# Weight pieces of a mixture-of-experts layer, issued by one queue or by two

## The chip, the cores and the metric

The kernel runs on one core of a Trainium2 chip. Its engines are named as in the profile: PE is TensorE (matrix products), DVE is VectorE, ACT is ScalarE, POOL is GpSimd and SP is SyncE, which here only waits and issues DMAs. A DMA that SP or ACT issues is carried out by the core's 16 DMA engines. The metric is the time of one execution in microseconds (us) of device time; less is better.

## The reference

One decoder layer for 256 tokens of width 1024, in float32: two attention mixers with gates, then a mixture of experts, then a final norm. Nearly all the bytes are in the experts. Each token goes to 4 of 32 experts, and each expert has three matrices of 1024 x 1024:

```python
def expert_block(args):
    xb, e = args
    g = xb @ w_gate[e] + b_gate[e]
    u = xb @ w_up[e] + b_up[e]
    g = jnp.minimum(g, SWIGLU_LIMIT)
    u = jnp.clip(u, -SWIGLU_LIMIT, SWIGLU_LIMIT)
    a = g * jax.nn.sigmoid(SWIGLU_ALPHA * g) * (u + 1.0)
    return a @ w_down[e] + b_down[e]
```

That is 32 x 3 x 4 MiB = 402.7 MB of expert weights, each byte read once, out of the 437.7 MB that the profile counts as read from memory.

## The kernel before

The first part (to about 228 us of the span) computes norms, projections, attention and the router. It is not touched. The second part runs over the 32 experts. An expert's tokens are gathered into 64 slots, and its three products are made on PE (line 1044), with the weights as the moving operand.

The weights come in **pieces** of 2 MiB: piece n is half of one matrix, 128 partitions with one run of 16 KB each. An expert has 6 pieces (gate 0 and 1, up 2 and 3, down 4 and 5), so there are 192, numbered 0 to 191. The order is given by the table ORDER: expert by expert, except that the last two experts have gate and up of both first, and then the two down matrices: pieces 188 and 189 for expert 30, 190 and 191 for expert 31. Piece 191 is cut into three DMAs.

The pieces go round a ring of 10 buffers (`RING = 10`): piece n lies in buffer n modulo 10. In the trace the buffers have the names pool (seven of them), attn, slot_wv and slot_gt; even buffers are pool_51, slot_wv, pool_50, pool_53 and slot_gt, odd ones attn, pool_49, pool_52, pool_54 and pool_55. Each buffer has its own semaphore `ld_ring`, on which PE waits before it uses the piece. When PE has finished a piece it adds one to `pieces_used`, and piece n may be issued when `pieces_used` is n - 9 or more.

Pieces 0 to 9 are issued by SP during the first part, as their memory falls free (line 369). All others are issued by SP in a loop (lines 421 to 428), in the order of n, each after its wait; so all pieces stand in one queue.

For every expert n, ACT does this, in this order: the sigmoid of the gate (`item_sigmoid`, line 621, after the gate product), the copy of the gathered tokens of expert n + 1 (`gathered_out`, line 629), for some experts the copy of a turned selection (line 625), the copy of the turned activation (`turned_activation`, line 634, which PE needs for the down product), and two copies of the expert's output (`item_out`, line 641, after the down product). The function `five` (line 644) writes this out for five experts; it is called six times, for experts 0 to 29, and `last_pair` does experts 30 and 31.

PE's order for an expert: gate product, gather of the next expert's rows (line 980), up product, turning of the gathered rows (line 700), combination of older outputs (line 1063), turning of the activation (line 700), down product. A product is 32 matmuls, 16 for each piece.

Of the kernel before, what the change touches and what calls it, by code (L numbers as in the profile page):

```python
# [35 lines left out]
E = 32  # L36
# [3 lines left out]
PIECES = 6  # L40
RING = 10
# [3 lines left out]
ORDER = [(e, m, j) for e in range(LAST) for m in range(3) for j in range(2)]  # L45
# [72 lines left out]
def layer(nc, x, ln_mix_g, w_in, b_gate_a, b_gate_b, w_o_a, w_o_b, w_out, ln_ffn_g, w_router, b_router,  # L118
# [6 lines left out]
    def sem(name):  # L125
        return ctx.enter_context(nc.semaphore(name))

    with ctx:
# [70 lines left out]
        ring = [attn[:, 8 * SEQ:24 * SEQ].rearrange("p (k c) -> p k c", c=D), slot_wv]  # L199
        ring = [pool[2]] + ring + [pool[0], pool[1], pool[3], pool[4], pool[5], slot_gt, pool[6]]  # L200
# [60 lines left out]
        ld_ring = [sem(f"ld_ring{s}") for s in range(RING)]  # L261
# [27 lines left out]
        pieces_used = sem("pieces_used")  # L289
# [17 lines left out]
        expert_v = [t[0].rearrange("e (j p r) f -> e j p r f", p=P, r=RUN) for t in (w_gate, w_up, w_down)]  # L307
# [48 lines left out]
        def _(sp):  # L356
# [61 lines left out]
            sp.wait_ge(prob_ready, NB)  # L418
            for q in range(4):
                sp.dma_start(b_dn[q], b_down[0][:, SEQ * q:SEQ * q + SEQ]).then_inc(ld_bdn, 16)  # L420
            for n in range(RING, E * PIECES):
                sp.wait_ge(pieces_used, n - RING + 1)
                if n == E * PIECES - 1:
                    for q, r in enumerate((slice(0, 2), slice(2, 3), slice(3, 4))):
                        sp.dma_start(ring[n % RING][:, r, :], expert_v[2][E - 1, 1][:, r, :]).then_inc(ld_last[q], 16)
                else:
                    expert, m, j = ORDER[n]
                    sp.dma_start(ring[n % RING][:], expert_v[m][expert, j]).then_inc(ld_ring[n % RING], 16)
# [32 lines left out]
        def _(act):  # L461
# [33 lines left out]
            for c in range(8):  # L495
                for b in range(NB):
# [6 lines left out]
                    else:  # L503
                        at, n = V_CHUNKS[c]
# [114 lines left out]
            def item_sigmoid(n):  # L619
                act.wait_ge(g_ready, n + 1)  # L620
                act.activation(sig, g_act, ACT.Sigmoid, scale=ALPHA).then_inc(sig_done, 1)  # L621

            def turned_selection(groups, slots=P, bank=DN):
                act.wait_ge(sel_turned, groups)
                act.activation(sel_t[0:slots], ps[0:slots, bank, 0:SEQ], ACT.Copy).then_inc(sel_t_ready, 1)

            def gathered_out(n):
                act.wait_ge(gathered, n + 1)
                act.activation(x_rows, ps[:, X, :], ACT.Copy).then_inc(x_rows_ready, 1)

            def turned_activation(n, dst=a_t):
                act.wait_ge(a_turned, n + 1)

                act.activation(dst.rearrange("p (h j) c -> p j h c", h=2),  # L634
                               ps[:, G, :].rearrange("p (j h c) -> p j h c", h=2, c=SLOTS), ACT.Copy)\
                   .then_inc(a_t_ready, 1)

            def item_out(n, side, y_group):
                act.wait_ge(pieces_used, n * PIECES + 6)
                for h in range(2):  # L640
                    act.activation(y_group[SLOTS * side:SLOTS * side + SLOTS, 512 * h:512 * h + 512],  # L641
                                   ps[SLOTS * h:SLOTS * h + SLOTS, DN, :], ACT.Copy).then_inc(y_ready, 1)

            def five(t):
                for j, members in enumerate(MEMBERS):
                    for side, i in enumerate(members):
                        n, group = t * FIVE + i, t * len(MEMBERS) + j
                        if n == 0:
                            act.wait_ge(prob_turned, 1)
                            act.activation(prob_t, ps[0:E, DN, 0:SEQ], ACT.Copy).then_inc(prob_t_ready, 1)  # L650
                        item_sigmoid(n)
                        gathered_out(n + 1)
                        if side == 0 and group:
                            turned_selection(group, SLOTS * len(MEMBERS[j - 1]))
                        turned_activation(n)
                        item_out(n, side, y_bufs[Y_OF[j]])

            def last_pair():
                item_sigmoid(LAST)
                gathered_out(LAST + 1)  # L660
                turned_selection(GROUPS - 1, SLOTS)
                turned_activation(LAST)
                item_sigmoid(LAST + 1)
                turned_selection(GROUPS, bank=X)
                turned_activation(LAST + 1, x_g)
                act.wait_ge(pieces_used, FIRST[LAST, 2] + 2)
                for h in range(2):
                    act.activation(y_bufs[0][0:SLOTS, 512 * h:512 * h + 512], ps[SLOTS * h:SLOTS * h + SLOTS, DN, :], ACT.Copy)\
                       .then_inc(y_ready, 1)
                act.wait_ge(pieces_used, FIRST[LAST + 1, 2] + 2)  # L670
                act.activation(y_bufs[0][SLOTS:P, 0:512], ps[0:SLOTS, U, :], ACT.Copy).then_inc(y_ready, 1)

            gathered_out(0)
            for t in range(TURNS):
                five(t)
# [3 lines left out]
            with act.If(count > 0):  # L679
                with act.Fori(0, count) as k:  # L680
                    n = k + E
# [964 lines left out]
```

## Time and profile before

| | us |
|---|---|
| median of 3 runs | 1140.96 |
| lowest, highest | 1140.94, 1174.47 |
| the profiled execution | 1140.3 |
| its span, first to last instruction | 1138.4 |
| PE busy in the span | 1090.7 (96%) |
| DVE, ACT busy | 307.0 (27%), 215.5 (19%) |
| DMA: bytes moved, mean rate over the span | 439.24 MB, 386 GB/s |

The profiled execution's own time is 1.9 us above its span. The share of the DMA engines is the time that their packets took, summed and divided by 16 engines; it can be a little over 1 where one packet begins before the one ahead has ended. "Us to landing" is the time from the issue of a DMA to the moment at which its last byte is in and its semaphore is set; it contains the wait behind older DMAs of the queue. The PE clock that was granted is 1.00 in nearly the whole span.

### The profile page before, as it was taken

To read this page: it belongs to the slowest core of one execution; us is meant where nothing else is said; L and a number is where in the kernel's file an instruction comes from. 1 tells how busy PE (TensorE), PEld (TensorE's weight loads), DVE (VectorE), ACT (ScalarE), POOL (GpSimd) and SP (SyncE) were. 2 spreads that over 40 slices of the span, in tenths; PEclk is the share of its full clock that TensorE was granted. 3 is DMA by queue.
4 is the path that set the end of the run, shared out by engine and by line. 5 is a ranking of instruction groups with operands and counts; after the bars stand their busy time and mean duration, and the time that the engine had idled before them with its cause. 6 is when DMAs were issued, how large, how long until landed. Compare 5 with 4: busy or idle time off the path is not lost.

```text
span 1138.4 us, 12258 instructions
## 1 busy us (share of the span) xinstructions
PE 1090.7 (96%) x5261; PEld 500.2 (44%) x5261; DVE 307.0 (27%) x689; ACT 215.5 (19%) x371; POOL 3.6 (0%) x11
## 2 busy tenths in 40 slices
PE   7999999999999999999999999999999999999997
PEld 6888889733343333333333333333333333333332
DVE  8566778411111111111111111111111111111122
ACT  5444656211111111111111111111111111111002
POOL 0000000000000000000000000000000000000000
PEclk9999999999999999999999999999999999999999
DMA  9854229999999999999999999999999999999995
GB/s 352 268 182 152 112 81 409 398 398 429 427 429 427 428 428 427 428 427 429 427 429 428 429 428 429 428 428 429 428 428 428 428 428 429 428 429 428 428 428 239
DMA packets 44841, 439.24 MB, mean 386 GB/s; under 512 B 3947, under 2 KB 5507, under 8 KB 20229
## 3 DMA queue, kind: packets, MB, share of 16 engines
q1 hardware_dynamic: 44788, 438.74, 92.2%
q8 instruction: 24, 0.39, 0.1%
q14 instruction: 13, 0.10, 0.0%
q10 hardware_dynamic: 16, 0.00, 0.0%
HBM read 437.68 MB, written 1.05 MB: 385 GB/s over the span
## 4 chain that ended last, share of the span: by engine, by line
PE 79%; DMA 15%; DVE 2%; ACT 1%; issue 1%; POOL 0%; DVEq 0%; ACTq 0%; POOLq 0%
PE ps L1044 48%; DMA pool<-in_w_up_dram 11%; PE ps L1063 5%; PE ps L700 5%; DMA pool<-in_w_down_dram 4%; PE ps L980 4%; PE ps L730 2%; PE ps L780 2%; PE ps L738 2%; PE ps L1028 2%; ACT o_t L634 1%; PE ps L833 1%; PE ps L834 1%; PE ps L835 1%; DVE w_lo L1225 1%
## 5 line engine op out<-in xcount | busy, mean ns | idle before, releaser
L1044 PE MATMUL ps<-pool,o_t 128*64 128x512 f32 x2144 | 481.3, 595 | 20.5 <-ACT o_t L634 12.8
L1044 PEld LDWEIGHTS ps<-pool,o_t 128*64 128x64 f32 x2144 | 150.3, 137 | 309.1 <-issue 282.1
L1496 DVE TENSOR_SCALAR v_tok<-ps 128x512 f32<-128x512 f32 x32 | 22.1, 692 | 504.3 <-PE ps L1044 504.3
L634 ACT ACTIVATE o_t<-ps 128x512 f32<-128x512 f32 x32 | 19.1, 597 | 315.8 <-PE ps L700 315.7
L641 ACT ACTIVATE attn<-ps 64x512 f32<-64x512 f32 x60 | 35.5, 592 | 217.7 <-PE ps L1044 217.0
L1044 PE MATMUL ps<-slot_wv,o_t 128*64 128x512 f32 x304 | 69.4, 598 | 4.4 <-issue 4.4
L1044 PE MATMUL ps<-slot_gt,o_t 128*64 128x512 f32 x304 | 69.4, 598 | 4.2 <-ACT o_t L634 4.1
L1044 PE MATMUL ps<-attn,o_t 128*64 128x512 f32 x320 | 72.2, 592 | 0.4 <-DMA attn<-in_w_up_dram 0.4
L1063 PE MATMUL ps<-attn,o_t 128*128 128x512 f32 (+1 forms) x152 | 71.6, 600 | 0.8 <-DVE attn L1569 0.8
L621 ACT ACTIVATE attn<-v_tok 128x512 f32<-128x512 f32 x32 | 20.2, 630 | 228.0 <-DVE v_tok L1496 228.0
L980 PE MATMUL ps<-xs,work 128*64 128x512 f32 x256 | 60.7, 593 | 0.0
L700 PEld LDWEIGHTS ps<-cst,work 128*128 128x128 f32 (+1 forms) x268 | 33.1, 173 | 44.2 <-issue 41.5
L1502 DVE TENSOR_SCALAR a_rows<-ps 128x512 f32<-128x512 f32 x32 | 22.1, 692 | 107.4 <-PE ps L1044 107.4
L700 PE MATMUL ps<-cst,work 128*128 128x128 f32 (+1 forms) x268 | 47.4, 296 | 1.0 <-DVE work L1315 1.0
L1044 PEld LDWEIGHTS ps<-attn,o_t 128*64 128x64 f32 x320 | 23.5, 137 | 45.8 <-issue 43.3
L1044 PEld LDWEIGHTS ps<-slot_wv,o_t 128*64 128x64 f32 x304 | 21.4, 136 | 40.0 <-issue 40.0
L1044 PEld LDWEIGHTS ps<-slot_gt,o_t 128*64 128x64 f32 x304 | 20.3, 136 | 40.7 <-issue 35.3
L833 PE MATMUL ps<-h_hi,w_hi 128*128 128x256 f32 x128 | 37.9, 296 | 0.0
L1063 PEld LDWEIGHTS ps<-attn,o_t 128*128 128x128 f32 (+1 forms) x152 | 26.5, 190 | 25.4 <-issue 22.4
L834 PE MATMUL ps<-h_lo,w_hi 128*128 128x256 f32 x128 | 36.1, 282 | 0.0
L835 PE MATMUL ps<-h_hi,w_lo 128*128 128x256 f32 x128 | 36.1, 282 | 0.0
L1456 DVE CAST pick_bias<-cst 128x128 fp32r<-128x128 f32 x32 | 7.3, 228 | 97.8 <-PE ps L1044 97.8
(195 smaller groups left out, 960.3 us busy)
## 6 DMA issues: line engine op xcount, KB each, us to landing
pool<-in_w_gate_dram SPq DMA_DIRECT2D x45, 2048.0 KB, 29.9
pool<-in_w_up_dram SPq DMA_DIRECT2D x45, 2048.0 KB, 28.8
pool<-in_w_down_dram SPq DMA_DIRECT2D x44, 2048.0 KB, 29.5
attn<-in_w_gate_dram SPq DMA_DIRECT2D x7, 2048.0 KB, 29.4
slot_wv<-in_w_up_dram SPq DMA_DIRECT2D x7, 2048.0 KB, 27.0
slot_gt<-in_w_down_dram SPq DMA_DIRECT2D x7, 2048.0 KB, 34.7
slot_gt<-in_w_up_dram SPq DMA_DIRECT2D x6, 2048.0 KB, 23.6
attn<-in_w_down_dram SPq DMA_DIRECT2D x6, 2048.0 KB, 27.4
```

The lines of the kernel that those rows point to most:

```text
L634: act.activation(dst.rearrange("p (h j) c -> p j h c", h=2), ps[:, G, :].rearrange("p (j h c) -> p j h c", h=2, c=SLOTS), ACT.Copy)\
L641: act.activation(y_group[SLOTS * side:SLOTS * side + SLOTS, 512 * h:512 * h + 512], ps[SLOTS * h:SLOTS * h + SLOTS, DN, :], ACT.Copy).then ...
L700: return pe.transpose(out_ap, in_ap, ident[0:n, 0:n])
L730: mm = pe.matmul(ps[:, bank, 0:n], h_lo[:, b, k, :], w_hi[:, c % 2, k, 0:n], start=False, stop=(last and k == KT - 1))
L738: mm = pe.matmul(ps[:, bank, 0:n], h_hi[:, b, k, :], w_lo[:, c % 4, k, 0:n], start=False, stop=(last and k == KT - 1))
L780: pe.matmul(ps[:, bank, 0:n], h_hi[:, b, k, :], w_hi[:, c % 2, k, 0:n], start=(k == 0), stop=False)
L833: pe.matmul(ps[:, t % 2, 0:SEQ], w_hi[:, c % 2, k, cut], h_hi[:, :, k, :], start=(k == 0), stop=False)
L834: pe.matmul(ps[:, t % 2, 0:SEQ], w_hi[:, c % 2, k, cut], h_lo[:, :, k, :], start=False, stop=False)
L835: mm = pe.matmul(ps[:, t % 2, 0:SEQ], w_lo[:, c % 4, k, cut], h_hi[:, :, k, :], start=False, stop=(k == KT - 1))
L980: mm = pe.matmul(ps[SLOTS * h:SLOTS * h + SLOTS, X, :], sel[:, b, :], xs[:, b, 512 * h:512 * h + 512], start=(b == 0), stop=(b == NB - 1), ...
L1044: mm = pe.matmul(ps[SLOTS * h:SLOTS * h + SLOTS, bank, :], lhs[:, k, :], ring[(at + j) % RING][:, r, 512 * h:512 * h + 512], start=(k == 0 ...
L1063: mm = pe.matmul(ps[:, Y + 2 * b + h, :], sel_t[0:slots, P * b:P * b + P], y_group[0:slots, 512 * h:512 * h + 512], start=(first and b == ...
```

## The change

The pieces with an odd number, from 11 to 189, are issued by ACT instead of SP. SP keeps the even ones from 10 to 190, and piece 191. The condition of each piece is the same as before, but ACT looks at it only where the instruction stands in its own order: for expert n, piece 6n + 11 behind the sigmoid, piece 6n + 13 behind the copy of the turned activation, and piece 6n + 15 behind the two output copies. ACT's DMAs go to a queue of its own, so each of the 16 DMA engines can hold packets of two queues.

```diff
@@ -418,7 +418,7 @@
             sp.wait_ge(prob_ready, NB)
             for q in range(4):
                 sp.dma_start(b_dn[q], b_down[0][:, SEQ * q:SEQ * q + SEQ]).then_inc(ld_bdn, 16)
-            for n in range(RING, E * PIECES):
+            for n in list(range(RING, E * PIECES, 2)) + [E * PIECES - 1]:
                 sp.wait_ge(pieces_used, n - RING + 1)
                 if n == E * PIECES - 1:
                     for q, r in enumerate((slice(0, 2), slice(2, 3), slice(3, 4))):
@@ -641,6 +641,11 @@
                     act.activation(y_group[SLOTS * side:SLOTS * side + SLOTS, 512 * h:512 * h + 512],
                                    ps[SLOTS * h:SLOTS * h + SLOTS, DN, :], ACT.Copy).then_inc(y_ready, 1)
 
+            def odd_piece(n):
+                act.wait_ge(pieces_used, n - RING + 1)
+                expert, m, j = ORDER[n]
+                act.dma_start(ring[n % RING][:], expert_v[m][expert, j]).then_inc(ld_ring[n % RING], 16)
+
             def five(t):
                 for j, members in enumerate(MEMBERS):
                     for side, i in enumerate(members):
@@ -649,11 +654,14 @@
                             act.wait_ge(prob_turned, 1)
                             act.activation(prob_t, ps[0:E, DN, 0:SEQ], ACT.Copy).then_inc(prob_t_ready, 1)
                         item_sigmoid(n)
+                        odd_piece(n * PIECES + RING + 1)
                         gathered_out(n + 1)
                         if side == 0 and group:
                             turned_selection(group, SLOTS * len(MEMBERS[j - 1]))
                         turned_activation(n)
+                        odd_piece(n * PIECES + RING + 3)
                         item_out(n, side, y_bufs[Y_OF[j]])
+                        odd_piece(n * PIECES + RING + 5)
 
             def last_pair():
                 item_sigmoid(LAST)
```

On SP every second piece drops out. This is the place behind the four small loads of the down biases, where the pieces from 10 on begin (pool_51 is piece 10, attn piece 11, slot_wv piece 12); a minus is a row that is gone:

```order
 L420 DMA work<-in_b_down_dram 32x256
 L428 DMA pool_51<-in_w_down_dram 128x4096
-L428 DMA attn<-in_w_down_dram 128x4096
 L428 DMA slot_wv<-in_w_gate_dram 128x4096
-L428 DMA pool_49<-in_w_gate_dram 128x4096
 L428 DMA pool_50<-in_w_up_dram 128x4096
-L428 DMA pool_52<-in_w_up_dram 128x4096
 L428 DMA pool_53<-in_w_down_dram 128x4096
-L428 DMA pool_54<-in_w_down_dram 128x4096
 L428 DMA slot_gt<-in_w_gate_dram 128x4096
```

Pieces 11, 13, 15 and 17 have left SP's order, and the ones between them stand next to each other.

On ACT the three DMAs of an expert stand between its activations. Before, an expert of the middle of the run and the start of the next:

```order
L621 ACTIVATE attn<-v_tok 128x512
L629 ACTIVATE work<-ps 128x512
L625 ACTIVATE o_t<-ps 128x256
L634 ACTIVATE o_t<-ps 128x4x2x64
L641 ACTIVATE attn<-ps 64x512 x2
L621 ACTIVATE attn<-v_tok 128x512
```

The same stretch of ACT after the change:

```order
L621 ACTIVATE attn<-v_tok 128x512
L647 DMA pool_49<-in_w_down_dram 128x4096
L629 ACTIVATE work<-ps 128x512
L625 ACTIVATE o_t<-ps 128x256
L634 ACTIVATE o_t<-ps 128x4x2x64
L647 DMA pool_52<-in_w_gate_dram 128x4096
L641 ACTIVATE attn<-ps 64x512 x2
L647 DMA pool_54<-in_w_up_dram 128x4096
L621 ACTIVATE attn<-v_tok 128x512
```

One DMA stands ahead of the copy of the gathered rows (L629), one behind the copy that PE needs for the down product (L634), and one behind the output copies.

The end of SP's pieces after the change, from piece 182 (slot_wv) on:

```order
L428 DMA slot_wv<-in_w_up_dram 128x4096
L428 DMA pool_50<-in_w_gate_dram 128x4096
L428 DMA pool_53<-in_w_up_dram 128x4096
L428 DMA slot_gt<-in_w_down_dram 128x4096
L428 DMA pool_51<-in_w_down_dram 128x4096
L425 DMA attn<-in_w_down_dram 128x2048
L425 DMA attn<-in_w_down_dram 128x1024 x2
```

These are pieces 182, 184, 186, 188, 190 and 191, the last one in its three parts; 183, 185, 187 and 189 have gone to ACT.

## Rows read from the trace of the kernel before

**Rows 1.** The page, the span in 40 equal slices: DMA share in tenths, rate.
```profile
DMA  9854229999999999999999999999999999999995
GB/s 352 268 182 152 112 81 409 398 398 429 427 429 427 428 428 427 428 427 429 427 429 428 429 428 429 428 428 429 428 428 428 428 428 429 428 429 428 428 428 239
```

**Rows 2.** The page, DMA queues: packets, MB, share of 16 engines.
```profile
q1 hardware_dynamic: 44788, 438.74, 92.2%
...
q10 hardware_dynamic: 16, 0.00, 0.0%
```

**Rows 3.** Windows, one stretch of the experts, columns as the first row says.
```profile
core 0: us, PE busy (x) PEld busy (x) DVE busy (x) ACT busy (x) POOL busy (x), PEclk, DMA share, GB/s
...
600.00:700.00 100.00, 97.02 (x430) 35.29 (x428) 16.76 (x37) 10.16 (x18) 0.00 (x0) 1.00 1.01 428
```

**Rows 4.** DMA issues of 230:300, 300:400, 500:600, 900:1000, in this order; last, us to landing.
```profile
pool<-in_w_up_dram SPq DMA_DIRECT2D x3, 2048.0 KB, 11.2
...
pool<-in_w_up_dram SPq DMA_DIRECT2D x6, 2048.0 KB, 14.2
...
pool<-in_w_up_dram SPq DMA_DIRECT2D x6, 2048.0 KB, 22.9
...
pool<-in_w_up_dram SPq DMA_DIRECT2D x4, 2048.0 KB, 42.6
```

**Rows 5.** The chain that ended last, 600:800: start, us, what (two down products).
```profile
609.81 7.09 PE ps L1044 x32
...
749.33 7.09 PE ps L1044 x32
```

**Rows 6.** The same chain, from 900 us to the end.
```profile
868.73 41.18 DMA pool<-in_w_up_dram
...
918.89 7.09 PE ps L1044 x32
...
1065.76 7.09 PE ps L1044 x32
...
1076.89 43.54 DMA pool<-in_w_down_dram
1120.44 0.14 issue
1120.57 7.10 PE ps L1044 x32
1127.67 0.02 issue
```

**Rows 7.** DMA packets of 12:30, then of 600:700.
```profile
DMA packets 3483, 6.98 MB, mean 388 GB/s; under 512 B 70, under 2 KB 86, under 8 KB 3482
...
DMA packets 2938, 42.80 MB, mean 428 GB/s; under 512 B 325, under 2 KB 325, under 8 KB 325
```

**Rows 8.** Timeline of SP: start, us, issues (pieces 11 and 13).
```profile
231.05 0.35 SPq L428 DMA_DIRECT2D attn<-in_w_down_dram  x1
...
240.84 0.33 SPq L428 DMA_DIRECT2D pool<-in_w_gate_dram  x1
```

**Rows 9.** DMA issues of 231:232 and 240:241, the same two pieces, us to landing.
```profile
attn<-in_w_down_dram SPq DMA_DIRECT2D x1, 2048.0 KB, 11.4
...
pool<-in_w_gate_dram SPq DMA_DIRECT2D x1, 2048.0 KB, 11.4
```

**Rows 10.** The page, a DMA of 2 MiB issued beside little else.
```profile
wd<-in_w_out_dram SPq DMA_DIRECT2D x2, 2048.0 KB, 7.5
```

**Rows 11.** Timeline of ACT, near 233, 243 and 626 us; in brackets, idle before.
```profile
233.06 0.63 ACT L621 ACTIVATE attn<-v_tok 128x512 f32<-128x512 f32 x1
...
243.10 0.60 ACT L634 ACTIVATE o_t<-ps 128x512 f32<-128x512 f32 x1 [8.93 <-PE ps L700]
...
625.11 0.63 ACT L621 ACTIVATE attn<-v_tok 128x512 f32<-128x512 f32 x1 [6.97 <-DVE v_tok L1496]
626.10 0.60 ACT L629 ACTIVATE work<-ps 128x512 f32<-128x512 f32 x1 [0.36 <-PE ps L980]
```

**Rows 12.** Timeline, issues near the start: one by ACT, two large ones by SP.
```profile
0.72 0.59 ACTq L462 DMA_DIRECT2D rows<-in_ln_mix_g_dram  x1
...
5.34 9.25 SPq L363 DMA_DIRECT2D wd<-in_w_in_dram  x2
```

**Rows 13.** Timeline of PE, the gathered rows of the next expert are turned.
```profile
633.61 0.75 PE L700 MATMUL ps<-cst,work 128*128 128x128 f32 x4
```

## The prediction

> **What bounds the kernel now.** I read the 40 slices first [rows 1]. From about 230 us to the end the DMA row stands at 9 and the rate at 427 to 429 GB/s, without a dip: the experts' weights stream without a pause. A window in the middle says the same: share 1.01, 428 GB/s, with PE busy 97.0 of 100 us [rows 3]. Two engines look full there, and which one sets the pace can't be read from shares.
>
> The landing times tell it [rows 4]. A 2 MiB DMA beside little else lands 7.5 us after its issue [rows 10], and at 428 GB/s it takes 2.097 MB / 428 GB/s = 4.9 us to move. In the expert part the time from issue to landing grows from 11.2 us to 14.2, 22.9 and at last 42.6 us. So PE frees buffers faster than the stream fills them, and the queue grows from under one piece, (11.2 - 7.5) / 4.9, to seven, (42.6 - 7.5) / 4.9. Pace for pace: five experts take PE 749.33 - 609.81 = 139.5 us when it never waits [rows 5]; their 30 pieces take the stream 62.9 MB / 428 GB/s = 147.0 us. PE begins with full buffers, loses that lead, and at 868.73 + 41.18 = 909.9 us it waits for a landing for the first time on the chain [rows 6]. From there five experts take 1065.76 - 918.89 = 146.9 us [rows 6], the stream's own pace. The last long link of the chain is the landing of piece 190 at 1120.44, and behind it 7.1 us of matmuls on pieces 190 and 191 [rows 6].
>
> So **the stream is the bound from 230 us to its end**, although PE hides it until 910. Pieces 10 to 191 are 182 x 2.097 = 381.7 MB, or 892 us at 428 GB/s. What slows the stream comes out in full. What speeds it up pays only until PE is the bound: PE idles (146.9 - 139.5) / 5 = 1.5 us per expert over (1120.4 - 909.9) / 29.4 = 7.2 experts, **10.6 us in all**, and no faster stream can give back more.
>
> **The change part by part.** It adds and removes no byte and no wait on a product; 90 issues move from SP to ACT.
>
> *The issues on SP.* 90 fewer. SP waits for PE nearly all the time; nothing gained: 0.
>
> *The issues on ACT.* An issue took ACT 0.59 us, and SP 0.33 to 0.35 [rows 12, 8]; I take 0.6 each, 1.8 us per expert. The one in front of the copy of the gathered rows: the sigmoid ends at 625.74, so the copy starts at 626.34 instead of 626.10, and PE wants it at 633.61 [rows 11, 13]; hidden. The one behind the copy for the down product is behind what PE waits for, and the one behind the output copies runs into an idle time of 6.97 us in front of the next sigmoid [rows 11]; hidden. If this cover were gone, each of 30 experts would pay up to 0.6 us, 18 us, but only beyond the 1.5 us that PE then waits for the stream anyway. A long queue can also hold the issuing engine: SP needed 9.25 us for two issues near the start [rows 12], with 2 KB packets, 64 per DMA engine in each full transfer and over 200 outstanding. A piece is 128 packets of 16 KB, 8 per engine, and at most 9 pieces are outstanding, 72 per engine. I price this at 0.
>
> *Late issues.* ACT issues piece 6n + 13 behind the copy for the down product, some 3 to 5 us later than SP did. That costs only where the queue runs dry, so at the start, where it holds less than a piece. Piece 11 was issued at 231.05 and landed 11.4 us later, at 242.4 [rows 8, 9]; with 7.5 us for a lone piece it would have been in time at 234.9. ACT reaches it behind the sigmoid, at 233.7 + 0.6 = 234.3 [rows 11]. Piece 13 landed at 240.84 + 11.4 = 252.2, and could be issued until 244.7; ACT does it at 243.7 + 0.6 = 244.3 [rows 8, 9, 11]. Both are in time by 0.4 to 0.6 us, and later ones have more. Bounds: 0, and 2 us if each misses by one microsecond; I take 0.
>
> *The rate with two queues.* The trace shows nothing of it: the second queue carried 16 packets in all, q1 everything else [rows 2]. I bound it by what a packet costs beyond its bytes. In 600:700 there are 2938 - 325 = 2613 packets of 16 KB, so an engine spends 100 x 16 / 2613 = 612 ns on one. In 12:30 there are 3483 - 86 = 3397 packets of about 2 KB, 18 x 16 / 3397 = 84.8 ns on one [rows 7]. The difference, 527 ns for 14,336 bytes, is 27.2 GB/s per engine, 435 for sixteen; 9.4 ns per packet are left over. If the other queue's packet filled that gap, the stream would be 9.4 / 612 = 1.5% faster, 13.7 us, of which PE lets through 10.6. If changing queue made the gap twice as long, it would cost 13.7 us. The far end below is the 388 GB/s of the 2 KB packets [rows 7]: 381.7 / 388 = 984 us, 92 us more. I take 0, by the row that is nearest, the same pieces and buffers at 428 GB/s [rows 3].
>
> The Trainium skill speaks against the change here: DMA: Bandwidth & Descriptors, section "Rules for kernel authors", says that spreading DMAs over the issuing engines brings no bandwidth, since all run on the same 16 DMA engines. By that rule this term is 0 and the sum below stays; the rows alone leave it open between -10.6 and +92. No row here shows two queues at once.
>
> *The end.* Today pieces land 4.9 us apart in the order of use: 190 at 1120.4, and 191 at about 1125.3. With two queues served alike, SP's 190 and ACT's 189 come in together. If that is at 1120.4, PE has 189, 190 and 191 before it, 3 x 3.55 = 10.6 us (7.10 us is two pieces [rows 6]), and ends at 1131.1 instead of 1127.7: +3.4. If 188 and 189 come in together at 1115.5, it works through four pieces, 14.2 us, to 1129.7: +2.0. I take +2.7. Bounds: 0, and +8.2 if ACT's queue lags and 189 is last, at 1125.3 + 10.6 = 1135.9. Inside the stream, an even piece that shares its time with an odd one makes PE wait, but the stream loses nothing, since an engine goes on with the other queue.
>
> The same page, section "Queues, rings and completion order", says that a DMA engine takes turns between the queues it has work for, a packet from each. By it the even sharing holds, and the end costs 2.0 to 3.4 us. Nothing in a trace with one queue can show it.
>
> **Sum**: 0 + 0 + 0 + 0 + 2.7 on the profiled execution's 1140.3 us is 1143.0. The median of the runs is 1140.96, 0.7 above that execution, which changes nothing: **1143 us**.
>
> **The rivals.**
>
> *The second queue fills the gap between packets.* For it: 9.4 ns per packet are there to be had. Against it: the share is already 1.01 [rows 3], so the next packet begins before the last has ended. It gives 1140.3 - 10.6 + 2 = 1132 us, and not less, for PE is then the bound.
>
> *Changing queue costs something on each packet* (the slower side). Its place is the packet stream of the 16 engines; each packet then follows one of another queue, from another place in memory. One gap more makes 1143 + 13.7 = 1157 us. Two (18.8 ns, one for the read and one for the write side) make 1143 + 27.4 = 1170 us. It decides from 14 ns per packet on, where 2.3% of 892 us, 20.7 us, are lost. For it: a packet here does cost more than its bytes. Against it: nothing that I can read.
>
> *ACT's queue lags.* Three of an expert's six pieces hang on ACT's order, and the last of them comes in last: 1140.3 + 8.2 + 2 = 1150.5 us. Against it: ACT's part of the queue is only four or five pieces, so it is emptied first.
>
> *The change does nothing to the packets*, because the engines drain one queue's DMA before the other's. Then the order is nearly that of before, and the time 1140 to 1141.
>
> **How the numbers follow.** Unchanged rate, with either order: 0.55 (0.45 for 1143, 0.10 for 1141). Gap filled: 0.17. ACT's queue lags: 0.07. One gap more: 0.08. Two gaps or worse: 0.12. That leaves 0.01 for a gain that PE's floor does not let me derive. The range goes from 1131, under the filled gap, to 1160, over one gap more; it leaves out 0.13, and some of the cases' own spread. A change of 2%, 22.8 us, is about what a measurement of this kernel can tell from none: faster 0.01, within 0.86, slower 0.13. The forecast is no change.
>
> **What would show it.** In the changed kernel's slices the rate is again 427 to 429 GB/s from 230 us on: 433 would be the filled gap, 421 one more gap, 414 two. The DMA queues show half of the pieces' bytes each. The issues of ACT are spread between its activations without idle time of PE in front of the products that ACT's copies feed. Landing times of even and odd pieces differ by less than two pieces' time, and piece 189 lands before 191. The chain has the DMA's landing as its last long link and about 10 us of matmuls behind it instead of 7.1. I am wrong if the rate moves by more than half a per cent, or if the stream shows holes between 230 and 300 us.

## The result

The two-queue kernel takes 1142.89 us (median of 21 runs, 1140.85 to 1144.62) against 1140.57 us for the kernel before (21 runs), a ratio of 1.0021 with a 95% interval of 1.0015 to 1.0027. Two runs of the kernel before, at 1171.3 and 1174.5 us, fell in a slower state of the chip and are not in the ratio. The change costs 2.3 us, clear of the noise, and far inside 2%. The forecast was 1143. How much of its working holds is another matter, and it holds less than the sum suggests.

The page of the two-queue kernel: the slices, and the two hardware queues.

```profile
DMA  9854329999999999999999999999999999999995
GB/s 352 266 175 158 111 77 405 404 376 430 427 429 426 428 427 428 429 426 430 428 428 428 429 427 430 429 428 430 426 430 429 427 429 427 429 429 427 429 427 230
...
q1 hardware_dynamic: 31828, 249.99, 53.3%
q10 hardware_dynamic: 12976, 188.75, 39.0%
```

The change did what it says: q10, ACT's queue, now carries 188.75 MB (90 pieces), where it had 16 packets [rows 2]. The rate from 230 us on is what it was [rows 1]. One slice of that part differs clearly, the one from 228 to 257 us: 376 against 398.

That slice can be read more sharply. The profile counts bytes, so two runs can be compared at the same time after the same event. Each pair of rows here counts all packets from the start to 50 us, and then to 870 us, after piece 10's issue (at 228.13 us of the kernel before, at 228.92 of the two-queue kernel). The kernel before:

```profile
DMA packets 19009, 76.34 MB, mean 274 GB/s; under 512 B 1067, under 2 KB 2627, under 8 KB 16453
...
DMA packets 43116, 427.37 MB, mean 389 GB/s; under 512 B 3747, under 2 KB 5307, under 8 KB 19133
```

The two-queue kernel:

```profile
DMA packets 18971, 75.85 MB, mean 272 GB/s; under 512 B 1059, under 2 KB 2619, under 8 KB 16445
...
DMA packets 43076, 426.88 MB, mean 388 GB/s; under 512 B 3737, under 2 KB 5297, under 8 KB 19123
```

0.49 MB are missing at 50 us, and the same 0.49 MB at 870 us. So the stream lost 0.49 MB / 428 GB/s = 1.1 us once, near the start, and nothing in the 820 us behind it. Two queues cost no rate. The window of 4 us in which it was lost (columns as in [rows 3]), in the two-queue kernel:

```profile
246.00:250.00 4.00, 4.00 (x22) 1.61 (x20) 0.00 (x0) 0.00 (x0) 0.00 (x0) 1.00 0.91 319
```

The same window of the kernel before, 0.8 us earlier, since its first part was 0.8 us shorter in this profile:

```profile
245.20:249.20 4.00, 4.00 (x22) 1.63 (x20) 0.00 (x0) 0.00 (x0) 0.00 (x0) 1.00 1.03 436
```

The first part's length is no part of the change: piece 10 was issued between 228.1 and 229.5 us in the twelve profiles whose first part is the same, in no order that goes with what ACT issues.

The hole stands ahead of piece 13. ACT's timeline:

```profile
243.89 0.60 ACT L634 ACTIVATE o_t<-ps 128x512 f32<-128x512 f32 x1 [8.93 <-PE ps L708]
243.89 0.34 ACTq L647 DMA_DIRECT2D pool<-in_w_gate_dram  x1
```

SP had issued it at 240.84 [rows 8]; that is 241.6 on this kernel's clock, so ACT is 2.3 us late. The issue goes out while the activation in front of it still runs, both at 243.89; I had added the activation and the issue. It goes out 15.0 us after piece 10's issue, 1.2 us sooner than I had reckoned (244.3 - 228.1 = 16.2), and the hole is there all the same. The limit that I had worked out, 244.7 - 228.1 = 16.6 us, is therefore wrong. Part of the reason is in the landing time of piece 10, which has the stream nearly to itself:

```profile
pool<-in_w_down_dram SPq DMA_DIRECT2D x1, 2048.0 KB, 9.5
```

It took 9.5 us here and 9.4 in the kernel before, not the 7.5 of the DMA that I took for it [rows 10]. With 9.5 the limit would be 252.2 - 9.5 = 242.7 us of the kernel before, 14.6 us after piece 10's issue, and ACT would be 0.4 us late, where 1.1 us were lost. And 9.5 us is no constant: in the other profiles that load piece 10 whole it took 7.6 to 9.4 us. What goes with the issue is the count of bytes at 50 us. Where ACT issues piece 13 at 15.0 us after piece 10, and the issues around it stand as here (this kernel and four of the experiments below), it is 75.68 to 75.86 MB. Where SP issues it at 12.7 us (the kernel before and four experiments), it is 76.34 or 76.35 MB; one more experiment has SP issue it and lost bytes in another way, told below. So the last moment lies between 12.7 and 15.0 us; where exactly, and what sets it, the runs leave open.

### The profile page after: what moved, and what is told of

The parts are those of the page before. It is cut to its first block, busy times and chain, and to the rows that moved or that the text cites. A ratio compares the mean times of both kernels' runs of the same rounds, so it can differ in the third digit from the quotient of the medians.

```text
span 1141.0 us, 12258 instructions
## 1 busy us (share of the span) xinstructions
PE 1094.4 (96%) x5261; PEld 501.2 (44%) x5261; DVE 306.8 (27%) x689; ACT 215.4 (19%) x371; POOL 3.6 (0%) x11
## 3 DMA queue, kind: packets, MB, share of 16 engines
q10 hardware_dynamic: 12976, 188.75, 39.0%
## 4 chain that ended last, share of the span: by engine, by line
PE 80%; DMA 15%; DVE 2%; ACT 1%; issue 1%; POOL 0%; DVEq 0%; ACTq 0%; POOLq 0%
PE ps L1052 48%; DMA pool<-in_w_up_dram 15%; PE ps L1071 5%; PE ps L708 5%; PE ps L988 4%; PE ps L738 2%; PE ps L788 2%; PE ps L746 2%; PE ps L1036 2%; ACT o_t L634 1%; PE ps L841 1%; PE ps L842 1%; PE ps L843 1%; DVE w_lo L1233 1%; PE ps L927 1%
## 5 line engine op out<-in xcount | busy, mean ns | idle before, releaser
L634 ACT ACTIVATE o_t<-ps 128x512 f32<-128x512 f32 x32 | 19.1, 597 | 315.7 <-PE ps L708 315.6
L1052 PEld LDWEIGHTS ps<-slot_gt,o_t 128*64 128x64 f32 x304 | 20.3, 136 | 41.0 <-issue 35.6
L1071 PEld LDWEIGHTS ps<-attn,o_t 128*128 128x128 f32 (+1 forms) x152 | 26.5, 190 | 25.4 <-issue 22.4
L988 PEld LDWEIGHTS ps<-xs,work 128*64 128x64 f32 x256 | 18.1, 137 | 35.3 <-issue 34.8
```

The costliest lines, as they stand in the source:

```text
L634: act.activation(dst.rearrange("p (h j) c -> p j h c", h=2), ps[:, G, :].rearrange("p (j h c) -> p j h c", h=2, c=SLOTS), ACT.Copy)\
L988: mm = pe.matmul(ps[SLOTS * h:SLOTS * h + SLOTS, X, :], sel[:, b, :], xs[:, b, 512 * h:512 * h + 512], start=(b == 0), stop=(b == NB - 1), ...
L1052: mm = pe.matmul(ps[SLOTS * h:SLOTS * h + SLOTS, bank, :], lhs[:, k, :], ring[(at + j) % RING][:, r, 512 * h:512 * h + 512], start=(k == 0 ...
L1071: mm = pe.matmul(ps[:, Y + 2 * b + h, :], sel_t[0:slots, P * b:P * b + P], y_group[0:slots, 512 * h:512 * h + 512], start=(first and b == ...
```

## The end of the two-queue kernel

The landing times of pieces 187 to 190, in this order (issued at 1068.61, 1072.95, 1076.40 and 1080.39 us):

```profile
pool<-in_w_up_dram ACTq DMA_DIRECT2D x1, 2048.0 KB, 40.7
slot_gt<-in_w_down_dram SPq DMA_DIRECT2D x1, 2048.0 KB, 41.5
pool<-in_w_down_dram ACTq DMA_DIRECT2D x1, 2048.0 KB, 42.7
pool<-in_w_down_dram SPq DMA_DIRECT2D x1, 2048.0 KB, 41.1
```

They land at 1109.3, 1114.5, 1119.1 and 1121.5. Pieces of the two queues do not land in pairs, as I had assumed for the end: the queues run half a piece out of step, and landings stay 4.6 to 5.2 us apart. Only piece 190 comes sooner, when ACT's queue is empty behind 189. The chain of waits, at its end:

```profile
1068.61 40.65 DMA pool<-in_w_up_dram
1109.31 3.65 PE ps L1052 x16
1112.96 1.91 PE ps L1071 x4
1114.87 0.86 PE ps L708 x6
1115.73 13.92 PE ps L1052 x64
```

PE waits for piece 187 and for nothing behind it; the wait for piece 190, last link of the chain before [rows 6], is gone. The last product ends at 1129.65, 900.7 us after piece 10's issue; before, at 1127.67, 899.5 us after it. The difference is 1.2 us, the size of the hole, and nothing is left for the end. Two things cancel there. Counted from piece 10's issue, piece 187 lands at 880.4 us instead of 877.6, which is 1.6 us more than the hole explains. From its landing to the end of the last product it is 20.3 us instead of 21.9, since no wait for 190 follows.

## The experiments

Each time is compared with the kernel before, measured beside it; "before" is its median there.

**Pieces 11 to 29 back on SP.** These lines stand for all experiments that choose ACT's pieces by number: `by_act(n)` decides, `odd_piece` does nothing for the others, and SP's loop takes the rest in order.

```diff
+def by_act(n):
+    return n % 2 == 1 and 31 <= n <= 189
...
-            for n in list(range(RING, E * PIECES, 2)) + [E * PIECES - 1]:
+            for n in [n for n in range(RING, E * PIECES) if not by_act(n)]:
...
             def odd_piece(n):
+                if not by_act(n):
+                    return
```

> Pieces 11 to 29 go back to SP; ACT issues 31 to 189. Theory (one dry hole): the two-queue kernel moved 0.51 MB less by 250 us than the one before, counted from the same point, and never less than that later; 0.51 MB / 428 GB/s = 1.2 us, lost between pieces 12 and 13, and passed on in full. Then this kernel is 1.2 us faster than the two-queue one, 1141.7 us, with no hole at 245 to 250 us. Rival (the cost lies at the end, where 189 and 190 share the engines, 2.0 to 3.4 us as predicted): it stays at 1142.9.

Measured: 1141.82 us, ratio 1.0009 (0.9998 to 1.0021); before 1140.92. The median is where the theory had it, but the interval takes in both. The profile shows something else: no issue is late in it, and yet 0.64 MB are missing 30 us after piece 10's issue. PE's granted clock (last column but two) explains it, in three windows from 245 us:

```profile
245.00:248.00 3.00, 2.83 (x8) 1.09 (x10) 0.04 (x1) 0.08 (x1) 0.00 (x0) 0.52 1.01 429
248.00:251.00 3.00, 3.00 (x15) 0.95 (x13) 0.00 (x0) 0.00 (x0) 0.00 (x0) 0.91 0.92 393
251.00:254.00 3.00, 3.00 (x15) 0.93 (x11) 0.00 (x0) 0.05 (x1) 0.00 (x0) 1.00 0.91 273
```

The clock was at its lower level, 1.2 GHz, for about 3 us. Just ahead of it PE had two gaps, of 0.51 and 0.73 us, which the profiles of the kernel before and of the two-queue kernel have at the same place without a dip. The product took 8.73 us instead of 7.09, buffers came free late, and the stream ran dry behind it. The execution that was profiled took 1144.4 us, 2.6 above the median of its kernel; that the other runs had the dip is not shown. So this experiment does not decide between the theory and its rival.

**The last pieces back on SP.**

```diff
+    return n % 2 == 1 and 11 <= n <= 169
```

> Pieces 171 to 189 go back to SP; ACT issues 11 to 169. Rival (end): with the last pieces in one queue again the end costs nothing, 1140.2 to 1140.9 us, and piece 189 lands 4.9 us ahead of 190. Theory (dry hole): 1142.9 us as the two-queue kernel, since 189 landed at 1119.1 and three pieces of 3.5 us behind it end where the stream's delay of 1.2 us alone would have put them; the last matmuls end within 0.3 us of those of the two-queue kernel.

Measured: 1142.24 us, ratio 1.0011 (1.0002 to 1.0020); before 1140.92. The end is again one queue's: in the profile PE waits 1.33 us for piece 190 as before, at 1122.95. The last product ends at 1130.03, 901.0 us after piece 10's issue, where the two-queue kernel has 900.7. Undoing the end gained nothing in the profile. By the medians it is 1.3 us above its kernel before (0.2 to 2.3), the two-queue kernel 2.3 (1.7 to 3.1); the intervals overlap, and up to 1 us for the end stays possible. The time was 0.7 us under the theory's and 1.3 over the upper end of the rival's.

**Both.**

```diff
+    return n % 2 == 1 and 31 <= n <= 169
```

> Both: ACT issues only 31 to 169. If start and end are all that the second queue costs, this is the kernel before, 1140.6 us, ratio 1.000. A remainder, up to 1 us, would be something else: the span of the first part was 0.8 us longer in the two-queue profile before any piece was issued by ACT, and the stores at the end 0.6 us.

Measured: 1140.89 us, ratio 0.9995 (0.9986 to 1.0004). ACT issues 70 pieces between its activations, and some 650 us run on two queues, at no cost that the runs can see (1.6 us less to 0.5 more). The remainder of up to 1 us that I had allowed for is not there.

**Only piece 13 back on SP.**

```diff
+    return n % 2 == 1 and 11 <= n <= 189 and n != 13
```

> Only piece 13 goes back to SP; ACT issues all the other odd ones. Theory (one dry hole, made by the late issue of piece 13): the stream has moved as many bytes 50 us after the issue of piece 10 as in the kernel before (76.34 MB), and the time is 1.1 us below the two-queue kernel's, 1141.8 us. Rival (the hole comes with the second queue, whichever piece is late): 75.85 MB at that point and 1142.9 us.

Measured: 1141.36 us, ratio 1.0007 (0.9998 to 1.0016); before 1140.63. All bytes counted to 50 us after piece 10's issue:

```profile
DMA packets 19006, 76.34 MB, mean 274 GB/s; under 512 B 1064, under 2 KB 2624, under 8 KB 16450
```

That is the kernel before, to the last digit. One issue out of 90 makes the hole, and without it PE's last product ends at 1128.5, 899.5 us after piece 10's issue, the same as before. The hole's 1.1 us are shown. The median is 0.7 us above its kernel before, where the two-queue kernel is 2.3 above; whether these 0.7 us are anything, the interval (0.2 less to 1.8 more) leaves open.

**Late issues in the middle.** For experts 10 to 24 (`late`), two issues wait until the output copies are under way:

```diff
-                        odd_piece(n * PIECES + RING + 1)
+                        if not late:
+                            odd_piece(n * PIECES + RING + 1)
...
+                        if late:
+                            odd_piece(n * PIECES + RING + 1)
+                            odd_piece(n * PIECES + RING + 3)
                         odd_piece(n * PIECES + RING + 5)
```

> For experts 10 to 24, ACT issues pieces 6n + 11 and 6n + 13 only behind the output copies, together with 6n + 15: about 20 and 12 us later than SP would. Theory: the queue is 20 to 40 us deep there, the stream does not run dry and its rate stays 428 GB/s; and since an engine takes turns between the queues, a late piece in ACT's short queue lands 10 to 25 us after its issue, in time. So 1142.9 us as the two-queue kernel, within 1 us. Rival (late issues are paid for each time): 15 experts by 1 us or more, 1158 us or above.

Measured: 1151.76 us, ratio 1.0095 (1.0081 to 1.0108); before 1140.92. Theory and rival both missed. The stream lost nothing beside the two-queue kernel: 426.89 MB at 870 us, the two-queue kernel's 426.88. Still it is 9 us slower than that kernel.

**Late issues for experts 5 to 14.** The same edit with other numbers.

> As the late issue in the middle, which cost 9 us at a full stream rate, but for experts 5 to 14, where PE's lead is longer. Theory: late pieces cost when lateness plus time to landing passes the some 46 us that lie between a buffer's release and the use of its next piece; here it is 20 + 14 to 22 us, so PE waits for none of them, and the time is that of the two-queue kernel, 1142 to 1143.5 us. Rival (moving issues behind the output copies costs PE some 0.6 us per expert, whatever the lead): 6 us more, 1149 us.

Measured: 1156.59 us, ratio 1.0145 (1.0129 to 1.0161); before 1140.63. Both missed, the theory by more. The landing times of 900:1100, 200 us and more behind the last late issue, show what happened; ACT's pieces first, then SP's:

```profile
pool<-in_w_up_dram ACTq DMA_DIRECT2D x6, 2048.0 KB, 44.0
pool<-in_w_down_dram ACTq DMA_DIRECT2D x5, 2048.0 KB, 44.5
...
pool<-in_w_gate_dram SPq DMA_DIRECT2D x4, 2048.0 KB, 25.1
pool<-in_w_up_dram SPq DMA_DIRECT2D x4, 2048.0 KB, 23.3
```

The two-queue kernel, the same stretch:

```profile
pool<-in_w_up_dram ACTq DMA_DIRECT2D x6, 2048.0 KB, 43.4
...
pool<-in_w_up_dram SPq DMA_DIRECT2D x4, 2048.0 KB, 42.9
```

The late issues let SP's queue get ahead, and it stays ahead when they have ended. Both queues get half of the stream (2943 packets each in 900:1100) and both are asked for half of the pieces, so nothing brings them back into step. SP's pieces land (44.0 - 23.3) / 9.8 = 2.1 of their turns early and lie in the ring, landed and unused, while PE waits for ACT's. When the stream ends, PE has two more pieces' time to go than it should, half of the difference in landing: 10.4 us. With the dry holes, 427.37 - 424.88 = 2.49 MB or 5.8 us, that makes 16.2 us; measured are 16.0. This sum was made after the result; its test is the experiment "Late issues, then one queue". The late issues in the middle give (43.8 - 26.5) / 2 + 1.1 = 9.8 us; measured 10.8 (9.2 to 12.3).

**Late issues at the start**, experts 0 to 4.

> For experts 0 to 4, ACT issues pieces 6n + 11 and 6n + 13 only behind the output copies; piece 11 some 20 us and piece 13 some 8 us later than now. Theory (the stream bounds from 230 us on): there is less than one piece in the queue, the stream runs dry for about two pieces' time, 8 to 12 us, and although PE does not wait for a landing before 850 us the end is later by nearly all of it: 1150 to 1154 us. Rival (PE bounds until 910 us, and holes ahead of that are filled by its 10.6 us of slack): 1143 to 1145 us.

Measured: 1158.36 us, ratio 1.0159 (1.0144 to 1.0175); before 1140.63. The stream in 230:240 and 240:250:

```profile
230.00:240.00 10.00, 10.00 (x49) 3.13 (x47) 2.84 (x10) 2.77 (x4) 0.00 (x0) 1.00 0.69 233
240.00:250.00 10.00, 8.76 (x44) 4.00 (x42) 2.72 (x7) 0.60 (x1) 0.00 (x0) 1.00 0.57 211
```

427.37 - 423.42 = 3.95 MB are missing at the end, 9.2 us, in the 8 to 12 us that I had expected of the hole; and the queues are out of step by 44.1 - 29.5 = 14.6 us, 7.3 more. Sum 16.5, measured 17.7. The time is beyond my range of 1150 to 1154 us, which had nothing for queues out of step. PE's 10.6 us of slack absorbed nothing: the rival is out.

**Fewer bytes**, on the kernel before.

```diff
+                    rs = slice(0, 1) if n % 20 == 10 and n < 180 else slice(0, RUN)
-                    sp.dma_start(ring[n % RING][:], expert_v[m][expert, j]).then_inc(ld_ring[n % RING], 16)
+                    sp.dma_start(ring[n % RING][:, rs, :], expert_v[m][expert, j][:, rs, :]).then_inc(ld_ring[n % RING], 16)
```

> The kernel before, one queue; of 9 pieces (10, 30, ... 170) only the first quarter of the rows is loaded, so a small part of the weights is stale. It takes 9 x 1.573 = 14.2 MB, 33 us, out of the stream, the same products stay. Theory (PE's floor): PE is the bound to nearly the end and the time falls by 10.6 us, to 1130 us, and no more. Rival (the stream is the only bound): 1108 us.

Measured: 1131.12 us, ratio 0.9923 (0.9903 to 0.9943), 8.8 us less by the ratio, 6.5 to 11.1. Of 33 us taken out of the stream PE lets 9 or so through; the floor holds, and in 700:1000 PE waits for no landing.

**Late issues, then one queue.** As for experts 5 to 14, with

```diff
+    return n % 2 == 1 and 11 <= n <= 99
```

> As the late issue for experts 5 to 14, but ACT issues no piece beyond 99; from piece 100 on all are SP's. Theory (imbalance): the late issues left ACT's pieces 44 us in their queue and SP's 23 to 25, which keeps two landed even pieces waiting in the ring and puts PE 10 us behind the stream at its end; in one queue that goes away, since PE gains 1.5 us per expert on the stream. What stays is the dry hole near 370 us and the one near 250 us, 2.5 MB or 5.8 us: 1146.4 us. Rival (what PE has waited it does not get back): 1156.6 us as there.

Measured: 1146.62 us, ratio 1.0049 (1.0032 to 1.0065); before 1140.47. That is the theory's 1146.4, and the rival's 1156.6 is out. The 10 us of the queues out of step are gone; what is left are the holes (3.27 MB or 7.6 us in its profile; measured 6.2, from 3.7 to 7.4).

**Every tenth piece by ACT.**

```diff
+    return n % 10 == 1 and 11 <= n <= 181
```

> ACT issues only every tenth piece, 11, 21, ... 181 (those of the buffer attn), behind the sigmoid, the copy for the down product or the output copies as it comes; SP all others. Theory (an engine takes turns between the queues): ACT's piece has its queue to itself, gets half of the rate at once and lands 2 x 4.9 us plus 4 to 5 us, some 14 us, after its issue, however deep SP's queue is; SP's pieces land 40 us after theirs. Rival (packets go in the order of issue): ACT's lands as late as its neighbours, 40 to 45 us beyond 900 us. The time is 1140 to 1142 us either way.

Measured: 1142.82 us, ratio 1.0022 (1.0011 to 1.0034); before 1140.47. Landing times of 700:900:

```profile
pool<-in_w_up_dram SPq DMA_DIRECT2D x10, 2048.0 KB, 40.4
attn<-in_w_up_dram ACTq DMA_DIRECT2D x2, 2048.0 KB, 13.9
attn<-in_w_gate_dram ACTq DMA_DIRECT2D x2, 2048.0 KB, 13.8
```

ACT's piece passes (40.4 - 13.9) / 4.9, five to six pieces, that were issued ahead of it. The order of issue does not hold across the queues. The time is 0.8 us over my range's end. The pieces that are passed are the likely reason: counted from piece 10's issue, pieces 175 to 180 land 4.5 us later than in the kernel before and 182 to 189 0.4 us earlier. The last landing on the chain for which PE waits is that of 177, at 1061.81, and from there to the end of the last product PE is the bound. No run tests this.

**Small packets in two queues.** The kernel before, chunk 2 of the input weights issued by ACT:

```diff
-            for c in range(1, 4):
+            for c in (1, 3):
...
+            act.dma_start(slots[2][:, :, 0:V_CHUNKS[2][1]], win_v[:, :, CHUNK_COL[2]:CHUNK_COL[2] + V_CHUNKS[2][1]])\
+               .then_inc(ld_chunk[2], 16)
```

> The kernel before with one DMA moved: in the first part, where packets are 2 KB, chunk 2 of the input weights is issued by ACT behind its first conversions (about 13 us), so that from then to about 30 us both queues hold 2 KB packets. The cost that a packet has beyond its bytes is eight times as visible there: 388 GB/s with one queue in 12:30. If a second queue filled the 9.4 ns per packet, the rate would go towards 435 GB/s; if changing queue doubled them, towards 350. Theory (no effect, as with 16 KB packets, where it stayed 428): 380 to 395 GB/s while both queues are busy.

Measured in 16:24, when both queues are full of 2 KB packets; the time is 1141.44 us, ratio 1.0011 (1.0001 to 1.0022):

```profile
DMA packets 1530, 3.10 MB, mean 388 GB/s; under 512 B 16, under 2 KB 16, under 8 KB 1530
...
q1 hardware_dynamic: 764, 1.53, 52.9%
q10 hardware_dynamic: 766, 1.57, 52.5%
```

764 packets to 766, at 388 GB/s, where one queue had 388 in 12:30 [rows 7]. Neither 435 nor 350: the other queue's packet neither fills the 9.4 ns nor doubles them. The time is 1.0 us above its kernel before all the same (0.1 to 2.5). In the profile nothing of it lies in the experts' stream: piece 10 is issued at 229.8 us instead of 228.1, and the last product ends 898.9 us after that instead of 899.5. Why the first part is longer stays open.

## Why the prediction was right, and where it was not

- **The bound** (the stream from 230 us on, although PE does not wait before 910): right. The hole of 1.1 us near 250 us is there in full when the last product ends (1.2 us), and the cap of 10.6 us on any gain was measured as 8.8 (6.5 to 11.1).
- **The issues on SP and ACT**, 0 and 0: right. 70 of them beside the activations cost nothing. They cost even less than I assumed: an issue takes ACT 0.33 to 0.37 us instead of 0.6, and goes out beside the activation ahead of it.
- **Late issues**, taken as 0 with a bound of 2: the step that failed. The slack of 0.4 us for piece 13 rested on a lone landing time of 7.5 us, taken from a DMA of the output weights. The trace before had a better row for it: piece 10's own, 9.4 us. With it ACT comes out 0.4 us late; 1.1 us were lost, and the other 0.7 are not explained. The loss lies within the bound of 2. The prediction had called itself wrong if the stream showed holes between 230 and 300 us, and it shows one, 319 GB/s in 246:250.
- **The same step's reason** was wrong as well: that lateness costs only where the queue runs dry. Late issues beside a stream at full rate cost 9 us, by putting the queues out of step. The change itself escaped that: its ACT pieces land in 43.4 us and SP's in 42.9. Its issues are late by 0.7 us (6n + 11), 2.3 to 4.6 (6n + 13) and nothing (6n + 15), those of the late experiments by some 20 and 12; that the queues stay in step because of this is argued, not shown. What the late issues showed is in kind the rival of a lagging ACT queue, which I had at 0.07 and 1150.5 us: absent here, but 1151.8 to 1158.4 us there.
- **The rate**, 0: right, at 16 KB and at 2 KB. What the Trainium skill says in DMA: Bandwidth & Descriptors, section "Rules for kernel authors", that DMAs spread over the issuing engines gain no bandwidth, agrees with the traces: 428 GB/s in 900:1100 with one queue and with two. The gap rival and the slower rival are both out, their mechanism with them.
- **The end**, 2.7: mis-sized, and for a wrong reason. In the profiles it measured 0; the runs leave up to 1 us open. The turns that the Trainium skill describes in DMA: Bandwidth & Descriptors, section "Queues, rings and completion order", are borne out by 764 packets to 766. My use of them was not: turns do not make pairs, they keep whatever step the issues had. Nor was it "about 10 us of matmuls" behind the last long link, but 20.3 us of PE's work behind piece 187.
- **The sum**, 2.7 forecast and 2.3 measured: luck. There was 1.1 too little at the start and 2.7 too much at the end, by the profiles, and 1.2 us came on top that nothing in the working stands for. About half of the 2.3 is shown to be the hole; 1.2 us are not assigned, and the interval (1.7 to 3.1 us) is nearly as wide as that. The two profiles differ by 2.6 us: 0.8 ahead of piece 10, 1.2 from there to the last product, 0.6 behind it. Among the profiles the first varies by 1.4 us and the last by 1.1, in no order that goes with the change.

## What to carry to other kernels

Where a stream of DMAs is the bound, count bytes at the same time after the same event in both profiles: 0.49 MB named a 1.1 us loss that no digit of the page's busy rows showed. Splitting one ordered stream over two queues bought no rate here, with packets of 16 KB or of 2 KB, and it adds a state that one queue does not have: the two can get out of step, by some experts' late issues, and stay so until they are merged. If one does split it, issue the first pieces, while the queue is short, from the engine that does nothing else, and compare the landing times of both queues; in three experiments half their difference, with the holes, came within 0.2 to 1.2 us of what was lost.

## What the runs showed of the hardware

Two queues with work share the engines evenly: 764 packets to 766 in 8 us, and in windows of 0.2 us (17.5 to 18.3 us) 19 or 20 of one to 17 to 23 of the other, a little over one of each per engine. A DMA alone in its queue passes the five or six ahead of it in the other and lands in 13.8 us instead of 40. ACT issued a DMA in the same instant (243.89 us) as the activation in front of it began.

The granted clock of PE fell to its lower level for 3.4 us at a time in eight of the thirteen profiles, once or twice in the experts' part, and for 6.8 us once. At 245 us, where the queue was short, this cost the stream 1.5 us (0.52 in 245:248). The two-queue kernel's profile has it at 271 and 418 us, and so has the one with piece 13 back on SP; the byte counts show nothing of it in either, and the latter's last product ends where that of the kernel before does.
